# The low parts of two neighbouring weight units made by one VectorE operation of 2048 columns

## The chip, the cores and the metric

The kernel runs on one core of one Trainium2 chip. The metric is the device time of one launch in microseconds. The time shown for a kernel is the median of its runs.

## What is computed

One layer of an encoder block on 1024 tokens of width 1024, all in float32: an input projection, stick-breaking attention (8 heads), sliding-window attention (8 heads), an output projection, and then a mixture of experts, from which the change takes its place. Each token goes to 4 of 32 experts. An expert has a gate-and-up matrix of 1024 x 2048 and a down matrix of 1024 x 1024:

```python
gu = xb @ w_gate_up[e] + b_gate_up[e]
gate = jnp.minimum(gu[:, :D_FF], SWIGLU_LIMIT)
up = jnp.clip(gu[:, D_FF:], -SWIGLU_LIMIT, SWIGLU_LIMIT)
act = (up + 1.0) * (gate * jax.nn.sigmoid(SWIGLU_ALPHA * gate))
return act @ w_down[e] + b_down[e]
```

The results are weighted by the token's gates and added to the residual; an RMS norm ends the layer.

## The kernel before

**Stages.** Up to about 850 us of the span lie the projections, both attentions, the router and the tables of the expert loop. Then comes the expert loop, 33 passes, one for each item (an item is one expert with up to 192 of its tokens), and at last the final norm. The change touches the expert loop alone.

**Arithmetic.** A float32 product is made of three products in the type fp32r: high x high, high x low and low x high. The high part of a number is its cast to fp32r, and the low part is the rest. Activations are split in this way once for each item; the weights are split as they stream through.

**Units and the ring.** The 12 MB of an expert's weights are cut into 24 units of 128 rows x 1024 columns: units 0 to 7 belong to the first half of the hidden columns (gate and up together), 8 to 15 to the second half, 16 to 23 to the down matrix. The raw weights lie in gu_w and dn_w, filled by SyncE's queue. The high and the low parts go into a ring of 4 slots, w_high and w_low (RING = 4); unit u uses slot u % 4. Three engines work on each unit in turn:

- ScalarE (high_part, line 1146) waits for the unit's weights and for the counter unit_used, which says that unit u-4, the slot's last owner, has been used up by TensorE. Then it casts the raw unit into w_high and counts high_ready up.
- VectorE (low_part, line 1621) waits for high_ready, subtracts w_high from the raw weights into w_low, and counts split_ready up.
- TensorE (hidden, line 852, and down, line 869) waits for split_ready, runs the unit's six matmuls of 512 columns, and counts unit_used up.

SyncE loads the next expert's weights into a raw buffer once split_ready says that both units in that buffer have been split (refill, line 465; it waits for even counts).

**The order is written out by hand on each engine**, and each engine executes strictly in its order. VectorE, for one item (lines 1657 to 1690): low 0-3, select (three operations that build the next item's one-hot selection), low 4-9, read_slots (six tiny operations), low 10, clamp(0) (g_t and p_t out of PSUM, after unit 7), low 11, hidden_out(0) (two products; the second waits for the sigmoid), low 12-16, act_low_part(0), low 17-18, clamp(1) (after unit 15), low 19, hidden_out(1), the operations of overflow rows where the item has some, low 20-22, act_low_part(1), low 23, x_low_part (two operations, the next item's input).

ScalarE (lines 1221 to 1241): high 0-3, the scaled output of the previous item (y_sb), high 4-11, sigmoid(0), high 12-16, act_high_part(0), high 17-19, sigmoid(1), [overflow], high 20-22, act_high_part(1), [overflow], high 23, x_high_part (two). The sigmoid and the copies each bring a table load.

TensorE (lines 945 to 975): two bias matmuls, units 0-5, slots (16 short matmuls), units 6-7, two bias matmuls, units 8-12, turn_hidden(0) (four transposes, which wait for hidden_out(0)), units 13-15, over_hidden where there is overflow, units 16-19, turn_hidden(1), turn_rows (eight transposes of the next item's rows), units 20-22, over_out where there is overflow, unit 23.

An item with more than 128 tokens has overflow rows, which TensorE multiplies with the raw weights: over_hidden in 32-row strips (line 897) for up to 32 rows, in 64-row strips (line 903) above that, and over_out (line 918).

Of the kernel before, what the change touches and what calls it, by code (L numbers as in the profile page):

```python
# [7 lines left out]
ALU = mybir.AluOpType  # L8
# [11 lines left out]
KT = D // P  # L20
# [22 lines left out]
UNITS, RING = 3 * KT, 4  # L43
# [17 lines left out]
def program(nc, x, attn_norm, w_in, b_in, sb_out_norm, sw_out_norm, sinks, rel_bias_table, w_out, b_out,  # L61
# [11 lines left out]
    with ExitStack() as ctx:  # L73
# [3 lines left out]
        def at(name, shape, dtype, offset):  # L77
            return nc.alloc_sbuf_tensor_at(name, shape, dtype, offset=base + offset)

        def sem(name):  # L80
            return ctx.enter_context(nc.semaphore(name))
# [52 lines left out]
        gu_w = at("gu_w", [P, 2, KT, 2, HALF], F32, R)  # L134
        dn_w = at("dn_w", [P, FT, D], F32, R + 64 * KB)
# [30 lines left out]
        w_high = at("w_high", [P, RING, D], F32R, W)  # L166
        w_low = at("w_low", [P, RING, D], F32R, W + 16 * KB)
# [112 lines left out]
        high_ready, split_ready, unit_used = sem("high_ready"), sem("split_ready"), sem("unit_used")  # L280
# [22 lines left out]
        def blocks(u):  # L303
            i, _, kind = units[u]
            return i + 1 if kind == "sb" else min(i + 1, 2)
# [948 lines left out]
        def _(dve):  # L1254
# [153 lines left out]
            for u in range(NU + 1):  # L1408
# [3 lines left out]
                if u < NU:  # L1412
                    i, h, kind = units[u]
# [149 lines left out]
            def select(n, e, own, cls):  # L1563
                wide = [P, NT, P]
                own(dve.tensor_tensor(place[:], pos[:, :, bass.ds(e, 1)].rearrange("p t a -> p (t a)"),
                                      item_base[:, bass.ds(n, 1)].to_broadcast([P, NT]), ALU.subtract))
                places = place[:].unsqueeze(2).to_broadcast(wide)
                dve.tensor_tensor(sel[:, :, 0:P], cst[:, C_IOTA:C_IOTA + P].unsqueeze(1).to_broadcast(wide), places,
                                  ALU.is_equal)
                dve.tensor_tensor(sel[:, :, P:2 * P],  # L1570
                                  cst[:, bass.ds(cls * P + C_OVER, P)].unsqueeze(1).to_broadcast(wide), places,
                                  ALU.is_equal).then_inc(sel_ready, 1)

            def read_slots(n, own, cls):

                dve.wait_ge(slots_psum, n + 1)
                src = bank[:, 6, 0:16].rearrange("p (k c) -> p k c", k=2)
                places = scat_all[:, bass.ds(2 * n + 2, 2)]
                part = scat_all[:, bass.ds(2 * n + 3, 1)]
                own(dve.tensor_reduce(slot_f[:, :, 0], src[:, :, 0:2], AX.X, ALU.add))  # L1580
                own(dve.tensor_copy(gather_idx[:], slot_f[:, :, 0]))
                own(dve.scalar_tensor_tensor(slot_f[:, :, 1], src[:, :, 2], -1.0, cst[:, C_PAD_ROW:C_PAD_ROW + 2],
                                             ALU.add, ALU.mult))
                own(dve.tensor_tensor(places, slot_f[:, :, 0], slot_f[:, :, 1], ALU.subtract))
                own(dve.tensor_scalar(part, part, cst[:, bass.ds(cls + C_MUL, 1)], cst[:, bass.ds(cls + C_PART, 1)],
                                      ALU.mult, ALU.add))
                own(dve.tensor_reduce(gate_all[:, bass.ds(2 * n + 2, 2)], src[:, :, 3:6], AX.X, ALU.add))
                dve.sem_inc(slots_ready, 1)
# [21 lines left out]
            with dve.Fori(0, n_items) as i:  # L1610
                e_next = dve.value_load(item_tab[0:1, bass.ds(i + 1, 1)], min_val=0, max_val=NE - 1)
                cls_next = dve.value_load(item_tab[0:1, bass.ds(i + (2 * MAX_ITEMS + 1), 1)], min_val=0, max_val=1)
                n_tok = dve.value_load(item_tab[0:1, bass.ds(i + MAX_ITEMS, 1)], min_val=0, max_val=ITEM)
                done = [0]

                def own(ins):
                    done[0] += 1
                    ins.then_inc(dve_step, 1)
                    dve.wait_ge(dve_step, OWN * i + (start + done[0]))

                def low_part(us):
                    for u in us:
                        raw = (gu_w[:, u // KT, u % KT, :, :].rearrange("p g f -> p (g f)") if u < 2 * KT
                               else dn_w[:, u - 2 * KT, :])
                        dve.wait_ge(high_ready, UNITS * i + (u + 1))
                        dve.tensor_tensor(w_low[:, u % RING, :], raw, w_high[:, u % RING, :], ALU.subtract  # L1626
                                          ).then_inc(split_ready, 1)

                def clamp(h):
                    dve.wait_ge(unit_used, UNITS * i + (KT * h + KT + RING))  # L1630
                    dve.tensor_scalar(g_t[h][:], bank[:, 2 * h, :], LIMIT, None, ALU.min).then_inc(gate_ready, 1)
                    own(dve.tensor_scalar(p_t[h][:], bank[:, 2 * h + 1, :], LIMIT + 1, 1.0 - LIMIT, ALU.min, ALU.max))  # L1632

                def hidden_out(h):
                    own(dve.tensor_tensor(p_t[h][:], p_t[h][:], g_t[h][:], ALU.mult))  # L1635
                    dve.wait_ge(sig_ready, 2 * i + h + 1)
                    dve.tensor_tensor(p_t[h][:], p_t[h][:], s_t[:], ALU.mult).then_inc(act_ready, 1)

                def act_low_part(h):
                    dve.wait_ge(act_high_ready, 2 * i + h + 1)  # L1640
                    ks = slice(4 * h, 4 * h + 4)
                    dve.tensor_tensor(act_low[:, ks, :], bank[:, 2 * h, :].rearrange("p (k t) -> p k t", k=4),  # L1642
                                      act_high[:, ks, :], ALU.subtract).then_inc(act_split, 1)

                def over_rows(parts):
                    n = FF // parts
                    up = bank[:, 6, n:2 * n] if parts == 4 else bank[:, 7, :]
                    g, p, s = g_t[0][:, 0:n], p_t[0][:, 0:n], s_t[:, 0:n]
                    dve.tensor_scalar(g, bank[:, 6, 0:n], LIMIT, None, ALU.min).then_inc(over_gate, 1)
                    dve.tensor_scalar(p, up, LIMIT + 1, 1.0 - LIMIT, ALU.min, ALU.max).then_inc(over_step, 1)  # L1650
                    dve.wait_ge(over_step, OVER_OWN * i + 1)
                    dve.tensor_tensor(p, p, g, ALU.mult).then_inc(over_step, 1)
                    dve.wait_ge(over_step, OVER_OWN * i + 2)
                    dve.wait_ge(over_sig, i + 1)
                    dve.tensor_tensor(p, p, s, ALU.mult).then_inc(over_act, 1)

                low_part(range(4))
                dve.wait_ge(slots_psum, i + 1)
                select(i + 1, e_next, own, cls_next)
                low_part(range(4, 10))  # L1660
                dve.wait_ge(d_gather, 16 * i + 16)
                dve.wait_ge(d_gather_over, 16 * i + 16)
                read_slots(i + 1, own, cls_next)
                low_part(range(10, 11))
                clamp(0)
                low_part(range(11, 12))
                hidden_out(0)
                low_part(range(12, 17))
                act_low_part(0)
                low_part(range(17, 19))  # L1670
                clamp(1)
                low_part(range(19, 20))
                hidden_out(1)
                with dve.If(n_tok > P):
                    dve.wait_ge(over_psum, i + 1)
                    dve.sem_inc(dve_passed, 1)
                    with dve.If(n_tok > P + P // 4):
                        over_rows(2)
                    with dve.Else():
                        over_rows(4)  # L1680
                    dve.nop()
                with dve.Else():
                    dve.sem_inc(over_gate, 1)
                    dve.sem_inc(over_step, OVER_OWN)
                    dve.sem_inc(over_act, 1)
                dve.nop()
                low_part(range(20, 23))
                act_low_part(1)
                low_part(range(23, 24))
                x_low_part(i + 1)  # L1690
                assert done[0] == OWN, done[0]

# [66 lines left out]
```

## Time and profile before

| | us |
|---|---|
| median of 3 runs | 2455.11 (2450.6 to 2465.33) |
| the profiled execution, time | 2448.64 |
| its span in the trace | 2446.9 |
| TensorE busy (matmuls) | 2234.3 (91% of the span) |
| VectorE busy | 1840.7 (75%) |
| ScalarE busy | 1368.1 (56%) |
| GpSimd busy | 270.6 (11%) |
| mean granted clock of TensorE | 0.916 of full speed |

Busy time of one engine is the sum of its instructions' spans. Matmuls overlap one another in the records (each is written as about 0.39 us, and they start 0.23 us apart), so the share of TensorE overstates how full it is; distances between starts are the better measure. VectorE's and ScalarE's instructions too overlap a little where they follow each other without a wait: the distance from start to start is shorter than the duration. An "idle before" names what ended the idle time.

### The profile page before, as it was taken

To read this page: it belongs to the slowest core of one execution; us is meant where nothing else is said; L and a number is where in the kernel's file an instruction comes from. 1 tells how busy PE (TensorE), PEld (TensorE's weight loads), DVE (VectorE), ACT (ScalarE), POOL (GpSimd) and SP (SyncE) were. 2 spreads that over 40 slices of the span, in tenths; PEclk is the share of its full clock that TensorE was granted. 3 is DMA by queue.
4 is the path that set the end of the run, shared out by engine and by line. 5 is a ranking of instruction groups with operands and counts; after the bars stand their busy time and mean duration, and the time that the engine had idled before them with its cause. 6 is when DMAs were issued, how large, how long until landed. Compare 5 with 4: busy or idle time off the path is not lost.

```text
span 2446.9 us, 37721 instructions
## 1 busy us (share of the span) xinstructions
PE 2234.3 (91%) x11191; PEld 1647.5 (67%) x11192; DVE 1840.7 (75%) x2582; ACT 1368.1 (56%) x1706; POOL 270.6 (11%) x259
## 2 busy tenths in 40 slices
PE   6999999889889399898999999989999999999997
PEld 4888666666578267777767666676676676666674
DVE  4222666777868689999989888897897798776696
ACT  3101544455532267777767666676675676575573
POOL 1000000000012011111111111111110111010022
PEclk9999555687799599999999999999999999999996
DMA  5310200000023759998699697896894797695694
GB/s 155 80 51 1 78 1 1 1 1 1 1 95 113 262 172 387 354 344 320 222 331 342 231 320 270 281 383 222 281 385 163 268 371 262 215 380 191 217 323 156
DMA packets 229432, 503.53 MB, mean 206 GB/s; under 512 B 24310, under 2 KB 42020, under 8 KB 229316
## 3 DMA queue, kind: packets, MB, share of 16 engines
q1 hardware_dynamic: 215060, 460.64, 51.7%
q0 software_dynamic: 14320, 42.22, 6.9%
q8 instruction: 30, 0.49, 0.1%
q14 instruction: 22, 0.18, 0.0%
HBM read 467.93 MB, written 34.87 MB: 205 GB/s over the span
## 4 chain that ended last, share of the span: by engine, by line
PE 54%; DVE 21%; issue 19%; ACT 3%; DVEq 1%; DMA 1%; SPq 0%; POOL 0%; ACTq 0%; POOLq 0%
PE bank L882 12%; DVE w_low L1626 9%; PE bank L665 8%; PE bank L860 6%; PE bank L687 5%; PE bank L726 4%; PE bank L760 3%; PE bank L897 3%; PE bank L707 3%; PE bank L918 3%; PE bank L903 3%; DVE p_t L1635 2%; DVE tB L1331 2%; ACT w_high L1155 1%; DVE p_t L1632 1%
## 5 line engine op out<-in xcount | busy, mean ns | idle before, releaser
L1626 DVE TENSOR_TENSOR w_low<-gu_w,w_high 128x1024 fp32r<-128x1024 f32 x528 | 620.0, 1221 | 114.8 <-ACT w_high L1155 108.6
L1155 ACT CAST w_high<-gu_w 128x1024 fp32r<-128x1024 f32 x528 | 544.2, 1049 | 199.0 <-PE bank L882 102.0
L860 PE MATMUL bank<-w_high,x_high 128*128 128x512 f32 x1056 | 429.6, 407 | 48.0 <-DVE w_low L1626 46.0
L860 PE MATMUL bank<-w_high,x_low 128*128 128x512 f32 x1056 | 413.3, 391 | 0.0
L860 PE MATMUL bank<-w_low,x_high 128*128 128x512 f32 x1056 | 412.6, 391 | 0.0
L1626 DVE TENSOR_TENSOR w_low<-dn_w,w_high 128x1024 fp32r<-128x1024 f32 x264 | 316.2, 1221 | 20.6 <-ACT w_high L1155 15.3
L1155 ACT CAST w_high<-dn_w 128x1024 fp32r<-128x1024 f32 x264 | 273.9, 1051 | 91.5 <-PE bank L860 81.9
L860 PEld LDWEIGHTS bank<-w_high,x_high 128*128 128x128 f32 x1056 | 198.5, 188 | 123.1 <-DVE w_low L1626 86.3
L882 PE MATMUL bank<-w_high,act_high 128*128 128x512 f32 x528 | 216.5, 410 | 46.2 <-DVE act_low L1642 46.2
L860 PEld LDWEIGHTS bank<-w_high,x_low 128*128 128x128 f32 x1056 | 198.6, 188 | 44.7
L860 PEld LDWEIGHTS bank<-w_low,x_high 128*128 128x128 f32 x1056 | 199.1, 189 | 37.2
L882 PE MATMUL bank<-w_high,act_low 128*128 128x512 f32 x528 | 209.7, 397 | 0.0
L882 PE MATMUL bank<-w_low,act_high 128*128 128x512 f32 x528 | 209.6, 397 | 0.0
L687 PE MATMUL bank<-qkT 64*128 64x256 f32 (+3 forms) x320 | 176.7, 663 | 26.5 <-DVE tB L1333 25.8
L882 PEld LDWEIGHTS bank<-w_high,act_high 128*128 128x128 f32 x528 | 101.3, 192 | 90.9 <-DVE w_low L1626 50.8
L562 POOL DMA_INDIRECT residual_rows<-y_sb,scat_idx x33 | 66.3, 2009 | 756.7 <-ACT y_sb L1161 478.4
L882 PEld LDWEIGHTS bank<-w_high,act_low 128*128 128x128 f32 x528 | 101.3, 192 | 22.4
L687 PEld LDWEIGHTS bank<-qkT 64*128 64x128 f32 x320 | 69.9, 259 | 67.7 <-issue 34.4
L882 PEld LDWEIGHTS bank<-w_low,act_high 128*128 128x128 f32 x528 | 101.7, 193 | 19.6
L665 PE MATMUL bank<-hT_high,in_high 128*128 128x512 f32 x288 | 113.7, 395 | 0.6 <-DVE in_bias L1303 0.6
L508 POOL TENSOR_TENSOR st<-st,cst 128x1 f32<-128x1 f32 x40 | 33.7, 843 | 724.8 <-DVE st L1270 724.8
L665 PE MATMUL bank<-hT_high,in_low 128*128 128x512 f32 x288 | 112.8, 392 | 0.0
(230 smaller groups left out, 3461.2 us busy)
## 6 DMA issues: line engine op xcount, KB each, us to landing
gu_w<-in_w_gate_up SPq DMA_DIRECT2D x528, 512.0 KB, 11.2
dn_w<-in_w_down SPq DMA_DIRECT2D x132, 1024.0 KB, 14.9
w_st<-in_w_in SPq DMA_DIRECT2D x14, 512.0 KB, 4.4
xt<-in_x SPq DMA_DIRECT2D x8, 512.0 KB, 4.2
wo_sb<-in_w_out SPq DMA_DIRECT2D x2, 2048.0 KB, 12.3
x<-in_x SPq DMA_DIRECT2D x8, 512.0 KB, 4.4
residual_rows<-x SPq DMA_DIRECT2D x8, 512.0 KB, 2.6
h_rows<-h SPq DMA_DIRECT2D x8, 512.0 KB, 2.9
```

The lines of the kernel that those rows point to most:

```text
L665: mm = pe.matmul(bank[:, n % 4, :], a[:, k, :], b[:, k, cols], start=first, stop=last)
L687: mm = pe.matmul(bank[:, z_bank[u] + c0 // 512, 0:n], qkT[r0:r0 + HD, q_tile, i * P:i * P + P], qkT[r0:r0 + HD, k_tile, k0 + c0:k0 + c0 + ...
L707: mm = pe.transpose(bank[:, 4 + g % 2, P * (b % 4):P * (b % 4) + P], src[:, P * b:P * b + P], ident)
L726: mm = pe.matmul(bank[:, 6 if kind == "sb" else 7, c0:c0 + w], lhs, v_sb[:, t, v0:v0 + w], start=(b == 0), stop=(b == n - 1))
L760: mm = pe.matmul(bank[:, 2 * (t % 2) + half, :], a, b[:, k, cols], start=first, stop=last)
L860: mm = pe.matmul(bank[:, 2 * h + g, :], a[:, k, :], b, start=False, stop=last)
L882: mm = pe.matmul(bank[:, 4 + half, :], a[:, j, :], b, start=first, stop=last)
L897: mm = pe.matmul(bank[rows, 6, :].rearrange("p (g f) -> p g f", g=2), lhs, rhs, start=(k < 0), stop=(k == KT - 1))
L903: mm = pe.matmul(bank[rows, 6 + half, :], lhs, rhs, start=(k < 0), stop=(k == KT - 1))
L918: mm = pe.matmul(bank[m * q:m * q + m, 7, 0:n], overT[:, c0:c0 + m], dn_w[:, j, n * q:n * q + n], start=(j == 0), stop=(j == FT - 1))
L1155: act.copy(w_high[:, u % RING, :], src).then_inc(high_ready, 1)
L1626: dve.tensor_tensor(w_low[:, u % RING, :], raw, w_high[:, u % RING, :], ALU.subtract).then_inc(split_ready, 1)
```

## The change

One VectorE operation makes the low parts of two neighbouring units. It reads 2 x 1024 columns of the raw weights and 2 x 1024 of w_high and writes two neighbouring slots of w_low. It waits until both units' high parts are there, and counts split_ready up by 2 when it is done. The ring keeps its 4 slots, and ScalarE's, TensorE's and SyncE's programs are as before. As low_part now takes units in pairs from an even one on, VectorE's order moves: clamp(0) comes after low 11 and no longer after low 10; act_low_part(0) after low 15 (before: 16); clamp(1) after low 17 (before: 18); act_low_part(1) after low 21 (before: 22).

```diff
                 def low_part(us):
-                    for u in us:
-                        raw = (gu_w[:, u // KT, u % KT, :, :].rearrange("p g f -> p (g f)") if u < 2 * KT
-                               else dn_w[:, u - 2 * KT, :])
-                        dve.wait_ge(high_ready, UNITS * i + (u + 1))
-                        dve.tensor_tensor(w_low[:, u % RING, :], raw, w_high[:, u % RING, :], ALU.subtract
-                                          ).then_inc(split_ready, 1)
+                    for u in us[::2]:
+                        raw = (gu_w[:, u // KT, u % KT:u % KT + 2, :, :].rearrange("p k g f -> p k (g f)") if u < 2 * KT
+                               else dn_w[:, u - 2 * KT:u - 2 * KT + 2, :])
+                        at = u % RING
+                        dve.wait_ge(high_ready, UNITS * i + (u + 2))
+                        dve.tensor_tensor(w_low[:, at:at + 2, :], raw, w_high[:, at:at + 2, :], ALU.subtract
+                                          ).then_inc(split_ready, 2)
...
-                low_part(range(10, 11))
+                low_part(range(10, 12))
                 clamp(0)
-                low_part(range(11, 12))
                 hidden_out(0)
-                low_part(range(12, 17))
+                low_part(range(12, 16))
                 act_low_part(0)
-                low_part(range(17, 19))
+                low_part(range(16, 18))
                 clamp(1)
-                low_part(range(19, 20))
+                low_part(range(18, 20))
                 hidden_out(1)
...
-                low_part(range(20, 23))
+                low_part(range(20, 22))
                 act_low_part(1)
-                low_part(range(23, 24))
+                low_part(range(22, 24))
```

## Rows read from the trace of the kernel before

**Rows 1.** Groups of VectorE, whole span: busy us, mean ns; idle before, releaser.

```profile
L1626 DVE TENSOR_TENSOR w_low<-gu_w,w_high 128x1024 fp32r<-128x1024 f32 x528 | 620.0, 1221 | 114.8 <-ACT w_high L1155 108.6 <-DVE gate_all L1587 0.2
...
L1649 DVE TENSOR_SCALAR g_t<-bank 128x256 f32<-128x256 f32 (+1 forms) x14 | 7.0, 501 | 75.8 <-PE bank L903 43.5 <-PE bank L897 32.3
```

**Rows 2.** Busy time of each engine in three stretches, each one item.

```profile
core 0: us, PE busy (x) PEld busy (x) DVE busy (x) ACT busy (x) POOL busy (x), PEclk, DMA share, GB/s
1032.40:1073.60 41.20, 37.24 (x182) 29.60 (x181) 38.91 (x46) 31.40 (x34) 6.25 (x6) 1.00 0.93 331
...
1617.10:1659.90 42.80, 39.41 (x190) 31.28 (x189) 38.89 (x46) 31.84 (x35) 5.90 (x6) 0.96 1.04 381
1330.30:1381.50 51.20, 49.65 (x326) 33.90 (x325) 40.56 (x49) 32.59 (x37) 6.55 (x6) 1.00 0.59 203
```

**Rows 3.** Waits, whole span: engine, line, releaser: total us, times, longest.

```profile
DVE w_low L1626 <- ACT w_high L1155: 123.9, 121, 6.3
```

**Rows 4.** Waits inside one plain item, 1032.4 to 1073.5 us.

```profile
PE bank L882 <- DVE act_low L1642: 2.5, 1, 2.5
...
PE bank L860 <- DVE w_low L1626: 1.4, 2, 1.0
```

**Rows 5.** Timeline of VectorE in that item: start us, length us, what.

```profile
1032.27 0.16 DVE L1565 TENSOR_TENSOR place<-pos,item_base 128x8 f32 x1
...
1034.75 6.89 DVE L1626 TENSOR_TENSOR w_low<-gu_w,w_high 128x1024 fp32r<-128x1024 f32 x6
1041.56 0.15 DVE L1580 TENSOR_REDUCE slot_f<-bank 128x2 f32<-128x4 f32 x1
...
1043.52 1.23 DVE L1626 TENSOR_TENSOR w_low<-gu_w,w_high 128x1024 fp32r<-128x1024 f32 x1 [0.22 <-ACT w_high L1155]
1044.66 0.68 DVE L1631 TENSOR_SCALAR g_t<-bank 128x512 f32<-128x512 f32 x1
...
1045.98 1.23 DVE L1626 TENSOR_TENSOR w_low<-gu_w,w_high 128x1024 fp32r<-128x1024 f32 x1
...
1073.42 0.16 DVE L1565 TENSOR_TENSOR place<-pos,item_base 128x8 f32 x1
```

**Rows 6.** Timeline of VectorE ahead of the loop: one operation of 2048 columns.

```profile
833.85 2.28 DVE L1603 TENSOR_TENSOR bias_hl<-bias_raw,bias_hl 32x2048 fp32r<-32x2048 f32 x1
```

**Rows 7.** Timeline of TensorE in the same plain item.

```profile
1034.18 0.39 PE L860 MATMUL bank<-w_high,x_low 128*128 128x512 f32 x1
...
1047.26 0.50 PE L860 MATMUL bank<-w_high,x_high 128*128 128x512 f32 x1 [0.36 <-DVE w_low L1626]
...
1048.07 0.40 PE L860 MATMUL bank<-w_high,x_high 128*128 128x512 f32 x1
...
1055.98 0.39 PE L882 MATMUL bank<-w_high,act_high 128*128 128x512 f32 x1
...
1061.42 0.60 PE L866 MATMUL bank<-cst,p_t 128*128 128x128 f32 x4
...
1065.41 0.49 PE L882 MATMUL bank<-w_high,act_high 128*128 128x512 f32 x1 [2.52 <-DVE act_low L1642]
```

**Rows 8.** Timeline of ScalarE in the same plain item.

```profile
1034.61 1.06 ACT L1155 CAST w_high<-gu_w 128x1024 fp32r<-128x1024 f32 x1 [0.30 <-PE bank L860]
...
1045.38 0.63 ACT L1177 ACTIVATE s_t<-g_t 128x512 f32<-128x512 f32 x1 [0.66 <-DVE g_t L1631]
1045.92 4.09 ACT L1155 CAST w_high<-gu_w 128x1024 fp32r<-128x1024 f32 x4
...
1062.05 0.59 ACT L1181 CAST act_high<-bank 128x512 fp32r<-128x512 f32 x1 [0.68 <-PE bank L866]
...
1063.48 1.08 ACT L1132 CAST x_high<-bank 128x512 fp32r<-128x512 f32 x2
1064.90 1.28 ACT L1155 ACT_TABLE_LOAD   x1 [0.34 <-issue]
```

**Rows 9.** Timeline of TensorE shortly after the end-of-item stall, 42.8 us item.

```profile
1652.10 0.63 PE L882 MATMUL bank<-w_low,act_high 128*128 128x512 f32 x1
```

## The prediction

> **What bounds the kernel now.** I read the groups of VectorE first. The subtractions of line 1626 run 528 times on the gate-and-up weights, 16 an item, so there are 33 items, and 14 of them have overflow rows (line 1649) [rows 1]. Next, what one item costs. From the select of one plain item to that of the next it is 1073.42 - 1032.27 = 41.15 us [rows 5]; an item with overflow takes about 51 (ten of them) or 62.5 (four), and the surplus is TensorE's [rows 2]. In a plain item VectorE has instructions on it for 38.9 of 41.2 us [rows 2], nearly back to back; TensorE meanwhile waits 1.4 us for low parts and once 2.5 us for act_low(1) [rows 4]. So VectorE sets the pace of plain items, but with little room: six low parts in a row take 6.89 us, from start to start (6.89 - 1.22) / 5 = 1.134 us [rows 5], and TensorE takes (1061.42 - 1055.98) / 4 = 1.36 us for each unit [rows 7]. Over the span VectorE waited 124 us for casts [rows 3]: the chain through the ring is felt already.
>
> **What the change removes.** Twelve VectorE instructions an item. A subtraction of 1024 columns lasts 1.22 us, the nearest operation of 2048 columns 2.28 us [rows 6] (on 32 partitions and not 128, which I take as equal). An operation that needs no wait starts 1.22 - 1.134 = 0.09 us before the last one's recorded end, so a pair should occupy 2.20 us and not 2 x 1.134 = 2.27: 0.07 saved a pair, 0.8 an item, 27 us in all if VectorE alone set the time. Bounds for what a pair occupies: 2.11 (twice the overlap) to 2.27 (nothing saved).
>
> The Trainium skill ("VectorE: DVE Perf Modes", section "The TRN2 errata — SBUF-src ops pay a fixed extra latency per instruction") states 151 cycles per fp32 tensor_tensor whatever its length, paid once by a large tile. By it a pair saves 0.157 us, 62 us over 396 pairs; its durations (estimates 1.22 and 2.29 us) agree with the rows, but start to start the rows show only half of that cost.
>
> **What it adds** is a longer way through the ring. Now a unit's slot comes free, is cast (0.04 us to wake, 1.05), subtracted (0.04, 1.22) and used (0.05, and 1.53 until its last matmul ends): 3.9 us, while four units of TensorE take 5.4. For a pair the second unit's slot counts, and the subtraction and the use are of two units: 0.04 + 1.05 + 0.04 + 2.28 + 0.18 + 2.89 = 6.5 us for four units, over 5.4. (0.04: from the end of unit 2's last matmul, 1034.18 + 0.39, to the cast at 1034.61 [rows 7, 8]. 2.89 is 1.36 + 1.53. 0.18 is TensorE's restart: 0.05 to its first matmul after low 11, and three matmuls in 0.81 and not 0.68 us [rows 5, 7].) Where TensorE just ran dry or is at pace, it now stalls in every pair. VectorE's other operations run in these gaps only where they lie between pairs.
>
> **The chain of one item after the change**, followed through the written orders, each leg being what the next one must wait for:
> - A, VectorE: pairs (0,1) and (2,3), 4.40; select, 1034.75 - 1032.27 = 2.48 [rows 5]. Sum 6.88.
> - B: pair (4,5) 2.28 + restart 0.18; TensorE's units 4 and 5, 2.89; the cast of unit 9, whose slot is unit 5's, 1.13. Sum 6.48.
> - C: pair (8,9) 2.20; read_slots 1.74 (1041.56 to 1043.30, where the wait of 0.22 begins); pair (10,11) 2.20; now only clamp(0)'s first operation 0.68 + 0.04, for ScalarE has the sigmoid ahead of cast 12; sigmoid 0.54 (to the cast at 1045.92); casts 12 and 13, 1.01 + 1.05 + 0.04; pair (12,13) and restart 2.46 [rows 5, 8]. Sum 11.96.
> - D: unit 12, 1.36; the four transposes 0.44 (0.60 less the overlap of 0.16 that matmuls show); unit 13, 1.53; the cast of unit 17, 1.13; pair (16,17) 2.20; clamp(1), 1045.98 - 1044.66 = 1.32; pair (18,19) and restart 2.46; units 18 and 19, 2.72; 0.63 from the transposes to act_high(1) [rows 5, 7, 8]. Sum 13.79.
> - E, ScalarE, whose order does not change: act_high(1) and cast 23, 1.43 (1062.05 to 1063.48); x_high and the table load, 2.70 (to 1066.18); casts 0 and 1 of the next item, 2.10 [rows 8]. Sum 6.23.
>
> Together 45.34 us against 41.15: **+4.2 us**. The moves are in it: clamp(0) behind low 11 puts the sigmoid, and the casts 12 to 15 queued behind it on ScalarE, one subtraction later (the stall ahead of unit 12, now about 1 us, becomes about 2.7); clamp(1) and act_low(0) come a subtraction earlier and gain nothing, as casts 16 and 17 wait for TensorE. act_low(1) behind low 21 and not 22 shortens the stall of 2.5 us [rows 4] to about 0.5, the one gain; what is late next is pair (0,1), behind x_high and the table load. A chain counts no small gaps, so I take 4.3.
>
> **Overflow items.** Their extra work lies behind unit 15. Legs A to C and the start of D are the same and lose some 4 us by unit 16; behind it the overflow matmuls give both orders time to fill the ring, and TensorE, busy 49.65 of 51.20 us [rows 2], had no end-of-item stall that could shrink. I take 4.3 here too; bounds 2.5 (the ring fuller at the next item's head) and 5.
>
> **Queues at no cost.** SyncE refills after even counts of split_ready, so its waits end as before to within one subtraction; the loads take 0.93 of the DMA engines' time in 41.2 us [rows 2], and a slower item leaves more room. If that cover went, a late load would delay a cast at the item's head. GpSimd's gather follows read_slots, a few us later in a slower item; TensorE's row transposes, which wait for it, come some 20 us behind.
>
> **Sum.** 33 x 4.3 = 142 us on 2448.64, the profiled execution's own time (span 2446.9), gives 2591. That execution lies 6.5 us under the median of 2455.11; on the median's footing **2597 us**. A pair occupying 2.11 or 2.27 us moves eight terms of the chain by 0.09 or 0.07: -24 or +19 us. With the small gaps and the overflow bounds, 2550 to 2640.
>
> **Rivals.**
> - *VectorE stays the bound, faster.* Half the item's VectorE time is other work; with pairs it has 41.15 - 0.8 - some 1.7 of waits = 38.6 us of work, 6.4 for two pairs, about as long as the ring's 6.5. Were that work spread evenly, the ring would hide behind it and 27 us would be won: 2428. For it: VectorE is the fullest engine. Against: the work is clumped (pairs 4 to 9 and 12 to 15 run with nothing between), and the ring can't carry a lead across. It decides if TensorE is still fed when a pair begins. Chance 0.06. A further 0.01 for its stronger form, in which the whole difference of durations, 2 x 1.22 - 2.28 = 0.16 us a pair, is won: 63 us, 2392. That is what the skill's fixed cost would make of it.
> - *Half hidden.* The casts of both units are often ready early and some stalls merge with existing ones: 0 to +2.8 us an item, 2455 to 2548. The 2.5 us at the item's end is such a reserve, but only one of seven stalls meets it. Chance 0.09.
> - *The clock falls as well.* In the item of 42.8 us the granted clock is 0.96 [rows 2]; after the end-of-item stall matmuls last 0.63 us and not 0.39 [rows 9], the lower level (1.2 and not 2.4 GHz) for a few us, price 1.65 us. I count six such items of 33. New stalls up to 2.7 us ahead of unit 12 could make it happen in every item: 27 x 1.65 = 45 us more, 2642. Against: ahead of unit 12 no stretch of light transposes joins the stall, and the stall at the item's end shrinks. Chance 0.06.
> - *The pair does not do what it says,* for instance a 2048-column operation much dearer than 2.28 us: beyond 2640 too. Chance 0.02.
>
> **How the numbers follow.** The forecast keeps 0.76; with the half-hidden case's upper edge and the clock case's lower edge, 2550 to 2640 holds about 0.8. A change of about 1% (25 us) is what a measurement of this kernel can tell from none. Faster by over 1%: 0.07. Within 1%: the low end of half hidden, 0.02. Slower: 0.91.
>
> **What would show it.** Right: line 1626 396 times at about 2.28 us; plain items 45 to 46 us from place to place; VectorE busy about 30 us less over the span but its waits for casts well over 200 us (124 now); TensorE waiting for low parts ahead of units 0, 4, 10, 12, 16 and 18, the longest ahead of 12; the end-of-item wait for act_low(1) under 1 us. Wrong: items of 41 us or less with VectorE back to back (the ring is not the limit); pairs that occupy over 2.3 us; a granted clock under 0.9 in the loop; casts that wait for weight loads.

## The result, and the profile after

Median 2651.94 us (2650.6 to 2655.03, four runs) against 2457.28 us: ratio 1.0792, interval 1.0757 to 1.0828. The change makes the kernel 195 us slower. The direction is the forecast one; the time lies 12 us above the range's upper end.

From the page of the changed kernel, the engines' busy time and the groups that answer to [rows 1]:

```profile
span 2650.3 us, 37259 instructions
...
PE 2307.4 (87%) x11191; PEld 1667.1 (63%) x11192; DVE 1822.6 (69%) x2186; ACT 1366.8 (52%) x1706; POOL 288.4 (11%) x259
...
L1627 DVE TENSOR_TENSOR w_low<-gu_w,w_high 128x2048 fp32r<-128x2048 f32 x264 | 599.0, 2290 | 202.9 <-ACT w_high L1155 191.2
...
L860 PE MATMUL bank<-w_high,x_high 128*128 128x512 f32 x1056 | 452.0, 428 | 189.1 <-DVE w_low L1627 189.1
...
L1627 DVE TENSOR_TENSOR w_low<-dn_w,w_high 128x2048 fp32r<-128x2048 f32 x132 | 302.6, 2293 | 91.7 <-ACT w_high L1155 88.7
L882 PE MATMUL bank<-w_high,act_high 128*128 128x512 f32 x528 | 218.0, 413 | 35.8 <-DVE w_low L1627 25.8
```

Twelve operations an item are gone and twelve joined ones are left (264 + 132 = 396, 2.29 us each), and VectorE is busy 18 us less than the 1840.7 before (forecast: about 30). What came instead is in TensorE's idle time: ahead of the x_high matmuls it now waits 189 us for w_low. Waits over the whole span, beside the 123.9 us of [rows 3]:

```profile
DVE w_low L1627 <- ACT w_high L1155: 279.9, 195, 7.1
...
PE bank L860 <- DVE w_low L1627: 189.1, 122, 4.4
...
ACT s_t L1177 <- DVE g_t L1632: 99.2, 66, 2.7
...
DVE act_low L1643 <- ACT act_high L1181: 71.0, 66, 2.4
```

ScalarE's casts wait for TensorE to be done with the slot's last unit. The same view has, for slots last used by a gate-and-up unit, first the kernel before and then the changed one:

```profile
ACT w_high L1155 <- PE bank L860: 174.4, 350, 1.6
```

```profile
ACT w_high L1155 <- PE bank L860: 317.6, 378, 3.5
```

Three items by stretch (PEclk is the granted clock): a plain one with a fall of the clock, a plain one without, and one with overflow. They answer to [rows 2]:

```profile
core 0: us, PE busy (x) PEld busy (x) DVE busy (x) ACT busy (x) POOL busy (x), PEclk, DMA share, GB/s
1111.00:1158.50 47.50, 39.99 (x182) 30.40 (x181) 38.33 (x35) 31.43 (x34) 6.44 (x7) 0.96 0.85 287
1158.50:1204.40 45.90, 38.41 (x182) 29.09 (x181) 38.27 (x34) 31.39 (x34) 6.36 (x7) 1.00 0.88 297
1252.50:1309.90 57.40, 51.93 (x323) 35.16 (x321) 40.10 (x39) 33.07 (x37) 5.73 (x7) 0.97 0.43 138
```

From select to select, plain items take 47.5 to 48.1 us, except two at 45.94 and 46.50; before it was 41.15, and 42.8 in six. Items with overflow take 55.8 to 57.6 (the first 59.4) and 67.5 to 69.0. The granted clock fell to its lower level for a few us 28 times in the loop, against 6 times before.

TensorE in the item without a fall (each row is the first matmul after a stall; compare [rows 7]):

```profile
1163.30 0.50 PE L860 MATMUL bank<-w_high,x_high 128*128 128x512 f32 x1 [1.15 <-DVE w_low L1627]
...
1174.10 0.50 PE L860 MATMUL bank<-w_high,x_high 128*128 128x512 f32 x1 [1.22 <-DVE w_low L1627]
...
1179.65 0.50 PE L860 MATMUL bank<-w_high,x_high 128*128 128x512 f32 x1 [2.49 <-DVE w_low L1627]
...
1186.67 0.50 PE L882 MATMUL bank<-w_high,act_high 128*128 128x512 f32 x1 [0.80 <-DVE w_low L1627]
...
1190.25 0.50 PE L882 MATMUL bank<-w_high,act_high 128*128 128x512 f32 x1 [0.56 <-DVE w_low L1627]
...
1195.23 0.49 PE L882 MATMUL bank<-w_high,act_high 128*128 128x512 f32 x1 [0.61 <-DVE act_low L1643]
...
1202.37 0.50 PE L860 MATMUL bank<-w_high,x_high 128*128 128x512 f32 x1 [0.60 <-DVE w_low L1627]
```

These are units 4, 10, 12, 16, 18, 20, and 0 of the next item. The stall ahead of unit 12 is as long here as in the items whose clock falls. VectorE in the same item, for [rows 5]:

```profile
1158.69 1.23 DVE L1568 TENSOR_TENSOR sel<-cst,place 128x1024 bf16<-128x1024 f32 x1
...
1167.50 2.29 DVE L1627 TENSOR_TENSOR w_low<-gu_w,w_high 128x2048 fp32r<-128x2048 f32 x1 [1.87 <-ACT w_high L1155]
...
1171.75 2.29 DVE L1627 TENSOR_TENSOR w_low<-gu_w,w_high 128x2048 fp32r<-128x2048 f32 x1 [0.30 <-DVE gate_all L1587]
...
1177.30 4.49 DVE L1627 TENSOR_TENSOR w_low<-gu_w,w_high 128x2048 fp32r<-128x2048 f32 x2 [0.50 <-ACT w_high L1155]
...
1184.32 2.29 DVE L1627 TENSOR_TENSOR w_low<-dn_w,w_high 128x2048 fp32r<-128x2048 f32 x1 [0.72 <-ACT w_high L1155]
...
1187.90 2.29 DVE L1627 TENSOR_TENSOR w_low<-dn_w,w_high 128x2048 fp32r<-128x2048 f32 x1
...
1190.92 0.69 DVE L1638 TENSOR_TENSOR p_t<-p_t,s_t 128x512 f32<-128x512 f32 x1
1191.59 2.29 DVE L1627 TENSOR_TENSOR w_low<-dn_w,w_high 128x2048 fp32r<-128x2048 f32 x1
...
1204.63 1.23 DVE L1568 TENSOR_TENSOR sel<-cst,place 128x1024 bf16<-128x1024 f32 x1
```

The distance from 1158.69 to 1204.63 is the item, 45.94 us. The idle times of 1.87, 0.50, and 0.72 us ahead of subtractions are what counts here: the engine that hardly stood still in a plain item now waits for casts, and the casts wait for slots (174.4 us before, 317.6 now).

### The profile page after: what moved, and what is told of

Same layout as the page of the kernel before. It is cut to its first block and busy times, and to the rows that moved or that the text cites. A ratio compares the mean times of both kernels' runs of the same rounds, so it can differ in the third digit from the quotient of the medians.

```text
span 2650.3 us, 37259 instructions
## 1 busy us (share of the span) xinstructions
PE 2307.4 (87%) x11191; PEld 1667.1 (63%) x11192; DVE 1822.6 (69%) x2186; ACT 1366.8 (52%) x1706; POOL 288.4 (11%) x259
## 5 line engine op out<-in xcount | busy, mean ns | idle before, releaser
L1627 DVE TENSOR_TENSOR w_low<-gu_w,w_high 128x2048 fp32r<-128x2048 f32 x264 | 599.0, 2290 | 202.9 <-ACT w_high L1155 191.2
L1155 ACT CAST w_high<-gu_w 128x1024 fp32r<-128x1024 f32 x528 | 535.8, 1047 | 235.8 <-PE bank L860 168.7
L860 PE MATMUL bank<-w_high,x_high 128*128 128x512 f32 x1056 | 452.0, 428 | 189.1 <-DVE w_low L1627 189.1
L860 PE MATMUL bank<-w_low,x_high 128*128 128x512 f32 x1056 | 427.2, 405 | 0.0
L860 PE MATMUL bank<-w_high,x_low 128*128 128x512 f32 x1056 | 427.0, 404 | 0.0
L860 PEld LDWEIGHTS bank<-w_high,x_high 128*128 128x128 f32 x1056 | 207.0, 196 | 288.6 <-DVE w_low L1627 252.1
L1627 DVE TENSOR_TENSOR w_low<-dn_w,w_high 128x2048 fp32r<-128x2048 f32 x132 | 302.6, 2293 | 91.7 <-ACT w_high L1155 88.7
L860 PEld LDWEIGHTS bank<-w_low,x_high 128*128 128x128 f32 x1056 | 207.3, 196 | 36.4
L549 POOL DMA_INDIRECT xg<-h_rows,gather_idx x34 | 80.5, 2366 | 404.3 <-DVEq L1588 372.3
L665 PE MATMUL bank<-hT_low,in_high 128*128 128x512 f32 x288 | 112.9, 392 | 0.0
```

Of the source, the lines that this page charges most:

```text
L549: pool.indirect_dma_start(xg[:, 0], None, h2_dram, bass.IndirectOffsetOnAxis(ap=gather_idx[:, 0:1].bitcast(U32), axis=0)).then_inc(d_gathe ...
L665: mm = pe.matmul(bank[:, n % 4, :], a[:, k, :], b[:, k, cols], start=first, stop=last)
L860: mm = pe.matmul(bank[:, 2 * h + g, :], a[:, k, :], b, start=False, stop=last)
L1155: act.copy(w_high[:, u % RING, :], src).then_inc(high_ready, 1)
L1627: dve.tensor_tensor(w_low[:, at:at + 2, :], raw, w_high[:, at:at + 2, :], ALU.subtract).then_inc(split_ready, 2)
```

## The experiments

All are changes of the expert loop. "Loop" is the distance from the first select to the last in the profiled execution; it leaves out the stages ahead of it, whose length differs by up to 16 us from one execution to another. "Plain item" is the distance from one select to the next in items without overflow: the shortest, of those without a fall of the clock, and the median of all; the first distance, which lies ahead of the loop's first whole item, is left out of the shortest. Falls are those of the granted clock inside the loop.

| | median us | ratio to before (interval) | loop | plain item, clock full | plain item, usual | falls |
|---|---|---|---|---|---|---|
| before | 2457 | 1 | 1547.7 | 41.12 | 41.16 | 6 |
| changed | 2652 | 1.079 (1.076 to 1.083) | 1742.3 | 45.94 | 47.55 | 28 |
| e1 order alone | 2421 | 0.984 (0.981 to 0.987) | 1521.9 | 40.1 | 40.1 | 0 |
| e2 e1 + wait for both casts | 2545 | 1.036 (1.032 to 1.040) | 1645.6 | 43.1 | 44.65 | 24 |
| e3 e1 + release of both together | 2549 | 1.035 (1.032 to 1.039) | 1640.8 | 43.0 | 44.65 | 22 |
| e4 e1 + both | 2657 | 1.081 (1.077 to 1.084) | 1748.4 | 46.0 | 47.7 | 30 |
| e5 changed + filler | 2609 | 1.062 (1.058 to 1.066) | 1701.0 | 45.9 | 46.0 | 0 |
| e6 e1 + pair (12,13) | 2532 | 1.031 (1.027 to 1.035) | 1627.8 | 42.0 | 43.6 | 27 |
| e7 e1 + four pairs | 2434 | 0.991 (0.987 to 0.994) | 1533.9 | 40.2 | 40.5 | 0 |
| e8 e1, ring of 3 | 2723 | 1.112 (1.107 to 1.118) | 1816.9 | 47.0 | 48.6 | 48 |
| e9 before, act_low(1) moved | 2416 | 0.985 (0.978 to 0.992) | 1518.7 | 40.0 | 40.0 | 0 |
| e10 before, the other moves | 2442 | 0.996 (0.993 to 1.000) | 1548.2 | 41.20 | 41.26 | 5 |
| e11 before + filler | 2439 | 0.993 (0.990 to 0.996) | 1539.8 | 41.11 | 41.15 | 0 |

**e1: the order alone.** VectorE's order of the changed kernel, with the single subtractions of the kernel before:

```diff
-                    for u in us[::2]:
+                    for u in us:
...
-                        dve.wait_ge(high_ready, UNITS * i + (u + 2))
+                        dve.wait_ge(high_ready, UNITS * i + (u + 1))
...
-                                          ).then_inc(split_ready, 2)
+                                          ).then_inc(split_ready, 1)
```

> VectorE's order as in the changed kernel, but 24 subtractions of 1024 columns, each with its own wait and its own release. Ring theory (the loss is the longer way of a pair through four slots): the moves alone cost nothing; the end-of-item stall for act_low(1) shrinks by one subtraction, so plain items take 40.0 us and the time is about 2435. Order theory (the loss comes from clamp(0) and the sigmoid one subtraction later, with casts 12 to 15 queued behind): plain items 43 us or more, time 2520 or more.

Measured 2421 us, 40.1 us in plain items (40.4 where the next item has overflow rows), no fall. The moves are no loss but a gain of 1.6%; the time lies 14 us under the 2435 expected, some 10 of them the six falls that are gone. TensorE's two stalls of a plain item, ahead of unit 12 and of unit 20 (the latter 2.5 us in [rows 4]):

```profile
996.64 0.50 PE L860 MATMUL bank<-w_high,x_high 128*128 128x512 f32 x1 [1.58 <-DVE w_low L1626]
...
1011.20 0.49 PE L882 MATMUL bank<-w_high,act_high 128*128 128x512 f32 x1 [1.30 <-DVE act_low L1642]
```

**e2, e3, e4: the pair without the joined operation.** Three ways to give e1's single subtractions a part of the pair's conditions:

```diff
e2   -  dve.wait_ge(high_ready, UNITS * i + (u + 1))
     +  if u % 2 == 0:
     +      dve.wait_ge(high_ready, UNITS * i + (u + 2))
e3   -  ... .then_inc(split_ready, 1)
     +  if u % 2:
     +      low.then_inc(split_ready, 2)
e4      both of these
```

> Order as changed; two subtractions of 1024 columns, the first of which waits for both casts; each releases its unit by itself. Ring theory: the cast of the second unit is put into the ring's cycle, about half the loss: plain items 2.8 us over e1, time about 2530 with the clock as before. Rival (the operation of 2048 columns is what costs): no change from e1.

> Order as changed; two subtractions of 1024 columns, each waiting for its own cast, but both units are released only when the second is done. Ring theory: plain items 2.7 us over e1, time about 2525. Rival (the operation of 2048 columns is what costs): no change from e1.

> Order as changed; two subtractions of 1024 columns, the first waiting for both casts, both units released after the second: the changed kernel without the joined operation. Ring theory: slower than the changed kernel by what the joined operation saves, 0.07 us on each of 8 pairs of the chain: plain items 0.5 us over its own, time about 2668. Rival (the joined operation costs more than two): faster than the changed kernel, 2600 or less. Clock theory (the falls of the clock come from the stall ahead of unit 12): at least 25 falls here too, fewer than 12 in e1.

With the clock full, plain items go from 40.1 us to 43.1 by the wait, to 43.0 by the release, and to 46.0 by both: 3.0 + 2.9 = 5.9, the changed kernel's item (45.94) but for 0.1 us. For e2, e3 and e4 it is the shorter of the only two plain items without a fall. So the loss of an item is all in when a pair may start and when it is handed over; that the operation is one and not two does next to nothing. The times of e2 and e3 came 15 and 24 us over what I had expected, for the clock fell 24 and 22 times and I had left it as before. The falls expected of e4 and e1 (at least 25, and fewer than 12) are there: 30 and none. I had expected e4 0.5 us an item above the changed kernel, and it is 0.1 to 0.2. Where the rest went, VectorE's timeline of e4 shows beside that of the changed kernel above:

```profile
1089.85 2.36 DVE L1627 TENSOR_TENSOR w_low<-dn_w,w_high 128x1024 fp32r<-128x1024 f32 x2
...
1092.93 0.69 DVE L1639 TENSOR_TENSOR p_t<-p_t,s_t 128x512 f32<-128x512 f32 x1
1093.54 2.35 DVE L1627 TENSOR_TENSOR w_low<-dn_w,w_high 128x1024 fp32r<-128x1024 f32 x2
```

Two subtractions here last 2.36 us together, the joined one 2.29, as forecast. But here the next subtraction starts 0.61 us after the product in front of it (1092.93 to 1093.54), and the joined one 0.67 us after it (1190.92 to 1191.59): there its later start gives most of the saving back. Behind read_slots it starts 0.07 us later, and behind the select of 1024 columns no later (1.13 us in both kernels).

**e5: filler in the stall ahead of unit 12.** The clock by itself:

```diff
-                hidden(i, 1, range(5))
+                hidden(i, 1, range(4))
+                filler(i, 8)
+                hidden(i, 1, range(4, 5))
...
+            def filler(i, n):
+                pe.wait_ge(y_ready, 2 * i + 2)
+                for _ in range(n):
+                    pe.matmul(bank[:, 7, :], x_high[:, 0, :], bias_hl[:, 0:HALF], start=True, stop=True)
```

> The changed kernel with eight extra matmuls of 512 columns (x_high times the bias, into bank 7, whose content nobody reads) between units 11 and 12 on TensorE, in the stall of 2.5 us. They take 8 x 0.23 = 1.8 us of it and delay nothing. Clock theory (the falls of the granted clock, 28 in the loop against 6 before, come from the stall ahead of unit 12, and each costs about 1.6 us): under 6 falls, plain items 46.0 us and not 47.5, time 2652 - 22 x 1.6 = about 2615. Rival (the falls come from the sum of all stalls in an item): falls as in the changed kernel, time 2650 or more.

2609 us, no fall, every plain item at 46.0 (or 46.5, where the next item has overflow rows to transpose). The eight matmuls and the start of unit 12, and the stretch of that item with its granted clock of 1.00:

```profile
1121.68 1.97 PE L866 MATMUL bank<-bias_hl,x_high 128*128 128x512 f32 x8
1124.39 0.50 PE L860 MATMUL bank<-w_high,x_high 128*128 128x512 f32 x1 [0.74 <-DVE w_low L1634]
```

```profile
1108.00:1154.00 46.00, 40.17 (x188) 30.66 (x188) 38.32 (x33) 31.50 (x33) 6.49 (x6) 1.00 0.89 295
```

TensorE does more work and the kernel is 43 us faster than the changed one (41 in the loop): 28 falls at 1.5 us. The filler also makes the sum of an item's stalls smaller, so e5 alone does not exclude that the sum decides, the rival of the expectation. The other runs do: in e5 TensorE's stalls of over 0.4 us still add up to 5.6 to 6.3 us in a plain item, without a fall, while in e3 they add up to 4.4 to 5.0 us and in e6 to 3.8 to 4.6, with 22 and 27 falls. e3's longest stall, ahead of unit 12, is 2.0 us:

```profile
934.40 0.50 PE L860 MATMUL bank<-w_high,x_high 128*128 128x512 f32 x1 [1.97 <-DVE w_low L1626]
...
937.33 0.63 PE L860 MATMUL bank<-w_low,x_high 128*128 128x512 f32 x1
```

For comparison with e5, the same place in the changed kernel, in an item whose clock falls:

```profile
1084.58 0.50 PE L860 MATMUL bank<-w_high,x_high 128*128 128x512 f32 x1 [2.54 <-DVE w_low L1627]
...
1085.63 0.54 PE L860 MATMUL bank<-w_low,x_high 128*128 128x512 f32 x1
...
1088.53 0.63 PE L860 MATMUL bank<-w_high,x_high 128*128 128x512 f32 x1
...
1089.51 0.39 PE L860 MATMUL bank<-w_high,x_high 128*128 128x512 f32 x1
```

Unit 12 starts at the full rate after the stall of 2.54 us, a us later the matmuls take 0.63 us, and at 1089.51 they are back at 0.39. In some other items of this run the first matmul of unit 12 is itself slow (0.74 to 0.80 us in six of them).

**e6, e7: which pairs cost.** Joined subtractions only for some units, all else as e1:

```diff
-                    for u in us[::2]:
+                    us = list(us)
+                    while us:
+                        n = 2 if us[0] in (12,) else 1        # e7: (6, 10, 20, 22)
+                        u, us = us[0], us[n:]
```

> VectorE's order as changed, single subtractions (as e1, plain items 40.1 us), but the one pair (12,13) joined. Ring theory: this pair alone adds the cast of unit 13 and a second subtraction ahead of unit 12, where the sigmoid has already made ScalarE late: plain items 41.6 us with the clock full, and overflow items 52.5; if the stall also makes the clock fall, 43.2; time 2470 to 2525. Rival (pairs cost only where several follow each other, one alone is absorbed by the ring): 40.1 us, 2421.

> As e1, but the pairs (6,7), (10,11), (20,21) and (22,23) joined: those behind which TensorE is held by something else (units still in the ring, the slots matmuls, the transposes, act_low(1)). Ring theory: no stall is added and 0.07 us is saved on each of four operations that VectorE must issue: plain items 39.8 to 40.1 us, time 2412 to 2421. Rival (each joined pair costs about a twelfth of the loss, 0.5 us): plain items 42 us, time 2485.

One pair alone, (12,13), costs 1.9 us an item at full clock and 106 us in the loop, 27 falls included, eleven of them twice as long as the others. TensorE's stall ahead of unit 12 is then 3.1 to 3.3 us, longer than at this place in any other run. In items with a long fall the unit starts at the slower rate at once, and in six items it starts at the full rate and no fall follows; one row of each kind:

```profile
1021.90 0.79 PE L860 MATMUL bank<-w_high,x_high 128*128 128x512 f32 x1 [3.25 <-DVE w_low L1630]
...
1244.15 0.50 PE L860 MATMUL bank<-w_high,x_high 128*128 128x512 f32 x1 [3.25 <-DVE w_low L1630]
```

The time is 7 us over the range I had given. e7 missed too, on the other side: the four pairs meant to be free are no gain; 2434 against e1's 2421, items 40.2 to 41.1. The wait of pair (10,11) for cast 11 is 0.33 to 0.38 us (0.22 for the single subtraction of e1), and that alone is more than the 0.07 us it saves. In items behind one with overflow rows the pair (6,7) too waits for a cast, about 0.5 us, where the single subtractions of e1 do not wait. Both in such an item:

```profile
1433.69 4.56 DVE L1630 TENSOR_TENSOR w_low<-gu_w,w_high 128x2048 fp32r<-128x2048 f32 x3 [0.47 <-ACT w_high L1155]
...
1440.25 2.29 DVE L1630 TENSOR_TENSOR w_low<-gu_w,w_high 128x2048 fp32r<-128x2048 f32 x1 [0.34 <-ACT w_high L1155]
```

**e8: a ring of three.** One constant of e1 changed (`UNITS, RING = 3 * KT, 3`).

> As e1 with single subtractions, but a ring of 3 slots. Ring theory (time is lost where the way from the freeing of a slot to the end of its next use is longer than TensorE's work on the ring's units): one way is 0.04 + 1.05 + 0.04 + 1.22 + 0.18 + 1.53 = 4.1 us against 3 x 1.36 = 4.1, with no reserve for VectorE's other operations: plain items 45 to 47 us with the clock full, the same kind of loss as the pairs with all 24 operations in place, time 2600 to 2680. Rival (the depth of the ring is not what costs): 2421.

47.0 us at full clock, and 48 falls; the median is above the range given, for the clock falls twice in many items. The longest stalls of a plain item stand ahead of the same units as in the changed kernel, 4 and 12 (there 1.15 and 2.5 us):

```profile
1006.05 0.50 PE L860 MATMUL bank<-w_high,x_high 128*128 128x512 f32 x1 [1.91 <-DVE w_low L1626]
...
1021.50 0.50 PE L860 MATMUL bank<-w_high,x_high 128*128 128x512 f32 x1 [1.99 <-DVE w_low L1626]
```

The other direction was not tried: by the same reasoning a ring of six would free the pairs, but the four slots fill the whole region that the kernel's layout gives the ring. That a deeper ring takes the loss away is argued and not shown.

**e9, e10: which move gains.** e9 is the kernel before with act_low_part(1) behind low 21 and not 22; e10 is e1 with act_low_part(1) back behind low 22.

> The kernel before with one of the moves: act_low(1) after low 21 and not after low 22. Theory (the gain of e1 is this move alone: it shortens TensorE's stall at the item's end by one subtraction, 2.5 to 1.3 us, and that also ends the falls of the clock there): plain items 40.1 us, no fall, overflow items as before, time as e1, 2421. Rival (the other moves bring it): 41.15 us, 6 falls, 2455.

> The kernel before with the other moves: clamp(0) after low 11, act_low(0) after low 15, clamp(1) after low 17, and act_low(1) left after low 22. Theory (act_low(1) is what counts): 41.15 us in plain items, about 6 falls, 2455. Rival: 40.1 us, 2421. My own reading of clamp(0) as a loss, with casts 12 to 15 behind the sigmoid, would show here as items of over 41.5 us.

e9 has the whole gain (40.0 us, 2416), e10 none in the loop (41.26 us and 5 falls, 1548.2 against 1547.7 us); its ratio of 0.996 lies at the edge of nothing. So the moved clamps cost 0.1 us an item with single subtractions.

**e11: filler in the kernel before.** Six matmuls ahead of unit 20 in plain items.

```diff
                 turn_extra_rows(i + 1, n_next)
+                with pe.If(n_tok > P):
+                    pe.nop()
+                with pe.Else():
+                    filler(i, 6)
+                pe.nop()
                 down(i, range(4, FT - 1))
```

> The kernel before with six extra matmuls of 512 columns (act_high times the bias, into bank 7, which nobody reads then) in plain items only, ahead of unit 20, in the stall of 2.5 us that waits for act_low(1); a branch is added on TensorE. Clock theory: the 6 falls go, each worth 1.65 us, 10 us in all, less some 0.1 us an item for the branch; plain items all at 41.2, time about 2447. Rival (the falls come from elsewhere): 6 falls stay, 2455 to 2460.

The six falls go, the plain items all take 41.1 to 41.2 us, and the loop is 8 us shorter. The median lies 8 us under what I had expected; the loop's length does not show why, and that stays open. Three of the six falls of before came behind a stall of 2.5 us ahead of unit 20 and three behind one of 1.9; in twelve other plain items the same two stalls brought none.

## Why the prediction was right or wrong

**Right: the ring is the loss, at the places named.** The chain of one item came to 45.34 us; the two plain items with the clock full show 45.94 and 46.50. The stalls came ahead of the units forecast: 4, 10, 12, 16, 18 and 0 with 1.15, 1.2, 2.5, 0.8, 0.6 and 0.6 us, the longest ahead of 12 (2.7 forecast). The stall for act_low(1) went from 2.5 to 0.6 us (0.5 forecast). e2 and e3 show the two halves of the longer way as two effects that add, 3.0 and 2.9 us; e8 shows the like loss from a shorter ring with nothing joined. The rival in which VectorE stays the bound fell with it: its waits for casts went from 124 to 280 us.

**Right: the price of the operation.** 2.29 us and 2.20 from start to start (4.49 - 2.29), as taken. By the section of the Trainium skill that I cited ("VectorE: DVE Perf Modes", "The TRN2 errata — SBUF-src ops pay a fixed extra latency per instruction") each pair would save 0.157 us, by estimate 1.3 us on the eight pairs of the chain. The runs show less: e4 stands 0.1 to 0.2 us an item over the changed kernel. The measurement decides: fewer and larger operations saved next to nothing here.

**Right in direction: the moves.** act_low(1) is the one that gains, as argued, 1.1 us in a plain item (e9). That clamp(0) behind low 11 costs by itself is hardly so: the stall ahead of unit 12 grows from 1.0 to 1.6 us, the item by 0.1 us (e10). In e6, where the pair (12,13) comes behind it, the item grows by 1.9 us; what that pair would cost with clamp(0) in its old place was not tried.

**Wrong: the clock.** The step that failed is the third rival, "The clock falls as well", which I gave a chance of 0.06, so that the sum has nothing for it, and in it the argument that "ahead of unit 12 no stretch of light transposes joins the stall". The clock fell 28 times, in items with a stall of 2.5 us there and nothing light in front of it. e5 fills this one stall and all the falls are gone, with the other six stalls left as they are. The price I had right: (47.55 - 45.94) = 1.6 us, against 1.65 from [rows 2]; 22 more falls are 35 us. I had read the six falls of before as belonging to stall and transposes together, while e11 shows only that filling the stall is enough; that the transposes matter was argued and not shown. And three of these six had followed a stall of 1.9 us, shorter than the 2.7 I forecast ahead of unit 12. What decides between an item with a fall and one without, at the same stall, no run shows.

**Mis-sized: the small gaps.** For a plain item I took 4.3 us over before, and it is 4.8 with the clock full. 0.30 of it is the gap ahead of the first subtraction behind read_slots (1171.75), whose like in [rows 5] I had left out of leg C as a wait of the old order. For the overflow items 4.3 was taken too; their distances without a fall give 4.8 to 5.2 (55.8 against 51.0, 67.5 against 62.3). The first whole item loses more, 6.5 us in e5, and I had no term for it.

The account, by the runs in which the clock never fell in the loop: e5's loop less that of e11 is 1701.0 - 1539.8 = 161 us, the longer way through the ring without any clock. The falls take 1742.3 - 1701.0 = 41 us in the changed kernel and 1547.7 - 1539.8 = 8 us before, 33 us more. Together 194 us, the 194.6 between the two loops. Forecast were 142 and nothing. Neither miss alone would have left the range: 161 us without the clock's 33 give 2618, and e5 itself has 2609; 142 with the 33 give 2632. The time lies 55 us over the forecast of 2597: 33 from the clock, 19 from the mis-sized item, and 2 from the median of before, which came out at 2457.28 and not 2455.11.

## What to carry to other kernels

Before joining two operations inside a ring of buffers, compare two sums: from the freeing of the last slot that the joined step needs, through all stages, to the end of its use, and the slowest stage's time for as many units as the ring holds. Here 6.5 us stood over 5.4, and the 0.07 us that a joined operation saves did not make up for it; the better kernel came from a move that shortened one wait (e9, 1.5% faster than before). And where a change opens a stall on TensorE as long as one behind which the clock is already seen to fall in the trace of before (1.9 and 2.5 us here), the fall belongs in the likeliest case of the forecast with its price, and not in a rival. How often it comes is the open part: behind such stalls it came in 6 of 18 plain items before and in 28 of 33 items after.

## What I had not expected of the hardware

- Stalls of 1.2 to 1.65 us ahead of a unit never brought the clock down in e1 (no fall in 33 items). Behind stalls of 2.0 us (e3) it fell in 22 items, behind the changed kernel's 2.5 us in 28, and behind 3.1 to 3.3 us (e6) in 27. In each of the three runs the next matmul already started slow in some items (0.79 us and not 0.50), and some items had the same stall and no fall.
- Eight matmuls an item, 1.97 us together, whose result nobody reads, made a kernel 43 us faster (e5).
- An operation of 2048 columns starts some 0.06 us later behind a short one than one of 1024 columns does (0.67 against 0.61 us behind the same product).
